# Forty-eight gathered tokens instead of thirty-two, eight tokens to a gather, and 136 sums to sort, in a two-block kernel's expert layer

## The chip, the cores and the metric

The kernel runs on one core of a Trainium2 chip (trn2), in one launch. The metric is the device time of an execution in microseconds; smaller is better. A core has a matrix engine (PE, whose weight loads are listed as PEld), a vector engine (DVE), a scalar engine (ACT), a general engine (POOL) and a queue engine (SP), each with its own instruction stream, tied together by semaphores. Transfers between memory and the on-chip buffer run on 16 DMA engines.

## The reference

Two transformer-like blocks on 256 tokens of width 2048. The change lies in the last part of the first block, the expert layer ("peer"). A token's query gives, in each of 8 heads, scores against two sets of 128 keys; the best 16 of each set are kept, the 256 pairwise sums are formed, and the best 16 sums name 16 of 16384 experts:

```python
v1, i1 = lax.top_k(s1, 16)
v2, i2 = lax.top_k(s2, 16)
cand = (v1[..., :, None] + v2[..., None, :]).reshape(T, 8, 256)
sv, si = lax.top_k(cand, 16)
expert = i1[si // 16] * 128 + i2[si % 16]
gate = softmax(sv)
a = gelu(einsum('cd,chkd->chk', x, exp_u[expert]))
out = einsum('chk,chkd->cd', gate * a, exp_v[expert])
```

`exp_u` and `exp_v` are 16384 x 2048 in float32. A token so uses 128 rows of each. The output goes back into the residual (x + g2 * out), is normalised, and enters the second block.

## The kernel before

**Weights as a stream.** All weight matrices come as units of 128 x 4096 floats (2 MB), 349 of them, in a fixed order. Behind `w_out` a unit is split into two float16 halves: SP loads it into one of two raw slots, ACT makes the high half (`hi`, L1840, two instructions), DVE the low half (`low`, L1077, two instructions), and PE multiplies (`product`, L530, L531, L532): high by high, high by low, low by high. There are two split slots: `hi` of unit n+2 waits until PE has used unit n, and PE starts unit n+2 when its `low` is done.

**Dense part.** Tokens 0 to 223 (DENSE_T = 224) go through all 16384 experts. The experts are cut into four quarters; quarter q has a stage uq (16 units, h times exp_u, gelu by ACT in `take_u`) and a stage vq (16 units, activations times exp_v, added to the residual by DVE in `residual_v`, L1573). The order is u0 u1 v0 u2 v1 u3 v2 v3. A unit is 96 matmuls of 224 columns. Gates get onto the activations by one-hot products: a routing step of 16 tokens is built by DVE (`hot`: L1547, L1549, L1553), multiplied by PE (`route`, L566, 32 matmuls), joined by DVE (`gated`, L1561), ACT (`route_high`, L2058) and DVE (`gated_low`, L1567). There are 14 steps a quarter (STEPS), one behind each of the first 14 units of u1, v0, v1 and v2. The first two `hot` of a quarter stand ahead of its stage.

**Gathered part.** Tokens 224 to 255 (ROWS_T = 32) go by gathered rows. For token i POOL issues a gather of its 128 rows of exp_u (1 MB, `row_load`, L2211) and a load that repeats its row of h on 128 partitions (1 MB, `h_load`, L2216); DVE takes the dot products (`row_dot`, L1511); ACT the gelu, DVE the weights (`row_weights`, L1519 to L1523); POOL gathers the 128 rows of exp_v, and PE sums them by four matmuls (`row_product`, L577). There is one h buffer, so `h_load(i)` waits for dot i-1. Dots lie in u2 (12, slots 2 to 13), u3 (12) and v3 (8), products in v1 (12), v2 (12) and v3 (8, from unit 6 on). At unit 12 of v3 ACT copies the sums out, PE transposes them at unit 13, and `add_rows` (DVE, L1530 to L1539) puts them into the residual at unit 14.

**Order.** Each engine's order is written out by hand: DVE's iteration n of a stage is `residual_v(n)` (v stages), `low(n+2)`, then the routing step, then (u2, u3) the dot. POOL's loads wait in order. The router's `select` runs on DVE in u0 as a generator of pieces, two or three a unit, and `top_keys` before it.

Of the kernel before, what the change touches and what calls it, by code (L numbers as in the profile page):

```python
# [54 lines left out]
ROWS_T = 32  # L55
# [129 lines left out]

def route_steps(n):

    return [n] if n < STEPS else []

ROW_GROUPS = [(0, 12), (12, 24), (24, 32)]
ROW_BATCHES = [(0, 12), (12, 24), (24, 28), (28, 32)]
ROW_LAST = {29: 0, 30: 1}


def row_loads():

    loads = []
    for n, (a, b) in enumerate(ROW_GROUPS):  # L200
        loads += [("u", i, i % 2) for i in range(a, b)]
        if n < 2:
            loads += [("v", i, i % 2) for i in range(a, b)]
        else:
            loads += [("v", i, ROW_LAST.get(i, 2)) for i in range(a, b)]
    place, count = {}, [0, 0, 0]
    for kind, i, buf in loads:
        count[buf] += 16
        place[kind, i] = (buf, count[buf])
    return place  # L210


ROW_PLACE = row_loads()
# [30 lines left out]
def program(nc, xT_d, wst, cst_d, dyn1_d, dyn2_d, dyn3_d, onehot_d, bmat_d, cmat_d, urow_d, vrow_d, skew_d, hrow_d, out_d):  # L244
    ctx = ExitStack()
    with ctx:
# [76 lines left out]
        def routed_half(q, n, r):  # L323
# [6 lines left out]
        h_row = J[0:ROWS_T, 0:2048]  # L330
        ident16 = dyn[:, 320:384].bitcast(F16)
        dots = small[:, 0:ROWS_T]
        row_w = [h_rep[:, 0:384], h_rep[:, 0:384], J[:, 6144:6272], J[:, 6272:6400]]
        row_w = [w.rearrange("p (i t) -> p i t", t=ROWS_T) for w in row_w]
        row_out = J[:, 2048:2560]
        row_tmp = J[:, 2560:3072]
        x_rows = X[:, :].rearrange("p (k t) -> p k t", k=KT)[:, :, DENSE_T:T]
# [13 lines left out]
        row_index = gates.rearrange("p q h c -> p (q h c)").bitcast(U32)[:, 0:ROWS_T]  # L351
# [3 lines left out]

        cand = J[:, 0:2048].rearrange("p (h a b) -> p h a b", h=HEADS, a=TOPK)
# [10 lines left out]
        pickT = W[:, 1024:1792].rearrange("p (f t) -> p f t", f=3)  # L367

# [3 lines left out]
        hot2 = [J[:, 4096 + 1024 * b:4096 + 1024 * (b + 1)].bitcast(F16).rearrange("p (t e) -> p t e", t=STEP_T)  # L372
                for b in range(2)]
        first1 = [J[:, 6144 + 256 * b:6144 + 256 * (b + 1)].bitcast(F16).rearrange("p (t e) -> p t e", t=STEP_T)
                  for b in range(2)]
        hot1 = [buf.bitcast(F16).rearrange("p (t r e) -> p t r e", t=STEP_T, r=2)
                for buf in (J[:, 6656:7168], dyn[:, 448:960])]
# [12 lines left out]
        def key_scores(h):  # L390
# [40 lines left out]
        row_in = [sem(f"row_in{i}") for i in range(3)]  # L431
# [4 lines left out]
            sem("rows_added"))  # L436
        merged, out_ready, relu_sb = sem("merged"), sem("out_ready"), sem("relu_sb")
# [49 lines left out]
        def _(pe_):  # L487
# [82 lines left out]
            def row_product(i):  # L570

                batch = [a <= i < b for a, b in ROW_BATCHES].index(True)
                buf, count = ROW_PLACE["v", i]
                pe_.wait_ge(row_w_ready, batch + 1)
                pe_.wait_ge(row_in[buf], count)
                for c in range(4):
                    mm = nc.tensor.matmul(psM[32 * c:32 * c + 32, 2, :], row_w[batch][:, i - ROW_BATCHES[batch][0], :],  # L577
                                          row_buf[buf][:, 512 * c:512 * c + 512], start=(i == 0), stop=(i == ROWS_T - 1))
                mm.then_inc(row_used, 1)

            def h_rows(c):
# [4 lines left out]
                for k in range(4 * c, 4 * c + 4):  # L586
                    for r in range(2):
                        mm = nc.tensor.matmul(psM[0:ROWS_T, 3, (k % 4) * P:(k % 4 + 1) * P], halves(H, k)[r][:, DENSE_T:T], ident16,
                                              start=(r == 0), stop=(r == 1))
# [362 lines left out]
            def turn_picks(qb):  # L952
                pe_.wait_ge(picked, qb + 1)
                if qb:
                    pe_.wait_ge(pickT_sb, 1)
                for f in range(3):
# [10 lines left out]
            for u in range(32):  # L967
# [3 lines left out]
                if u == 0:  # L971
                    key_head(7)
                for qb in range(2):
                    if u == 9 + 8 * qb:
                        turn_picks(qb)
                if u >= 16:
                    for step_n in route_steps(u - 16):
                        route(step_n)
                if 20 <= u < 24:
                    h_rows(u - 20)  # L980
            for q in range(4):
                v0 = FIRST[f"v{q}"]
                pe_.wait_ge(acts_ready, STEPS * (q + 1))
                for n in range(16):
# [5 lines left out]
                    if q in (1, 2) and 2 <= n < 14:  # L990
                        row_product(12 * q - 14 + n)
                    if q == 3 and 6 <= n < 10:
                        row_product(18 + n)
                    if q == 3 and n in (10, 11):
                        row_product(2 * n + 8)
                        row_product(2 * n + 9)
                    if q == 3 and n == 13:
                        pe_.wait_ge(row_out_sb, 1)
                        for j in range(4):
                            mm = nc.tensor.transpose(psM[:, 0, j * P:(j + 1) * P], row_out[:, j * P:(j + 1) * P], ident[:, :])  # L1000
                        mm.then_inc(row_T, 1)
                if q < 2:
                    stage(f"u{q + 2}", lambda s, j: unit_u(s, j), drained=False)
# [64 lines left out]
        def _(v):  # L1068
# [378 lines left out]
            def select(qb):  # L1447

                for h in range(HEADS):
                    D.put(tt(cand[:, h, :, :], val[qb][:, h, 0, :].unsqueeze(2).to_broadcast([P, TOPK, TOPK]),  # L1450
# [961 lines left out]
```

## Time and profile before

| | us |
|---|---|
| median of 3 runs (3352.15 to 3358.27) | 3352.95 |
| the profiled execution | 3353.19 |
| its span in the trace | 3351.3 |
| PE busy | 3231.2 |
| DVE busy | 2328.7 |
| ACT busy | 1236.4 |
| POOL busy | 319.9 |

The time of an execution lies about 2 us over its span. Times in the rows are microseconds from the span's start, unless marked ns. A busy PE is not PE at its peak, since matmuls are pipelined and their durations overlap; how fast it goes is read from the starts. The granted clock is a share of 2.4 GHz. The expert layer's eight stages run from 710.0 to 2029.1.

### The profile page before, as it was taken

Reading aid. Unit: us, or ns where it says so; the run is one execution under the profiler, and the core shown is the slowest. Engines: PE = TensorE matmul, PEld = TensorE weight load, DVE = VectorE, ACT = ScalarE, POOL = GpSimd, SP = SyncE. Lnnn points to the kernel's source line nnn. Section 1 sums busy time; section 2 is a strip of 40 time slices with the busy share of each in tenths; the row PEclk is TensorE's granted clock in tenths of the full one; section 3 lists DMA queues with packets and bytes.
Section 4 is the critical chain, followed back from the end, with each engine's and each line's share of the span. In section 5 each row is a group of like instructions: output and inputs, shape, how many; then the busy total and the mean of one; then the engine's idle time right before and its main releaser. Section 6 shows DMA issues by size and latency. Waiting matters only on the chain.

```text
span 3351.3 us, 70433 instructions
## 1 busy us (share of the span) xinstructions
PE 3231.2 (96%) x31230; PEld 2899.1 (87%) x31230; DVE 2328.7 (69%) x2654; ACT 1236.4 (37%) x1126; POOL 319.9 (10%) x278
## 2 busy tenths in 40 slices
PE   7999999999999999999999998999999999999998
PEld 4777768789899999999999887888888788888887
DVE  8596145799998966985698757578657655555554
ACT  2000142444444444434443324444443333343332
POOL 0275000000000002121212100210000000000000
PEclk8999999999999999999999999999999999999999
DMA  9657694446565569777978874555545455555553
GB/s 410 246 231 292 275 422 162 167 177 223 196 252 202 206 260 425 291 291 303 421 278 299 352 288 172 199 202 200 199 174 203 161 210 200 200 199 205 200 200 129
DMA packets 66046, 814.78 MB, mean 243 GB/s; under 512 B 7354, under 2 KB 9418, under 8 KB 10512
## 3 DMA queue, kind: packets, MB, share of 16 engines
q1 hardware_dynamic: 48528, 700.47, 54.8%
q0 software_dynamic: 15008, 109.10, 8.3%
q8 instruction: 174, 2.85, 0.3%
q10 hardware_dynamic: 2304, 2.10, 0.2%
q14 instruction: 32, 0.26, 0.0%
HBM read 807.71 MB, written 3.93 MB: 242 GB/s over the span
## 4 chain that ended last, share of the span: by engine, by line
PE 77%; DVE 12%; DMA 8%; issue 1%; ACT 1%; ACTq 0%; DVEq 0%; POOL 0%; SPq 0%; POOLq 0%
PE psW L530 20%; PE psW L531 20%; PE psW L532 20%; PE psW L528 7%; DMA proj<-h_rows 6%; DVE ring L1077 4%; DMA ring<-wst_dram 1%; PE psM L566 1%; PE psM L628 1%; PE psW L628 1%; DVE arena L1511 1%; PE psM L577 1%; PE psM L782 1%; DVE proj L1511 1%; DVE work L1405 1%
## 5 line engine op out<-in xcount | busy, mean ns | idle before, releaser
L1077 DVE SCALAR_TENSOR_TENSOR ring<-ring 128x2048 f16<-128x2048 f32 x526 | 1182.2, 2289 | 338.2 <-ACT ring L1840 336.3
L530 PE MATMUL psW<-h_act,ring 128*128 128x256 f16 (+1 forms) x5088 | 1366.4, 269 | 43.0 <-DVE ring L1077 20.2
L531 PE MATMUL psW<-h_act,ring 128*128 128x256 f16 (+1 forms) x5088 | 1366.1, 268 | 0.0
L532 PE MATMUL psW<-h_act,ring 128*128 128x256 f16 (+1 forms) x5088 | 1365.9, 268 | 0.0
L1840 ACT ACTIVATE ring<-ring 128x2048 f16<-128x2048 f32 x526 | 975.1, 1903 | 638.1 <-PE psW L532 548.6
L530 PE MATMUL psW<-arena,ring 128*128 128x224 f16 (+1 forms) x3072 | 812.4, 264 | 1.4 <-issue 0.9
L531 PE MATMUL psW<-arena,ring 128*128 128x224 f16 (+1 forms) x3072 | 812.2, 264 | 0.0
L532 PE MATMUL psW<-arena,ring 128*128 128x224 f16 (+1 forms) x3072 | 812.0, 264 | 0.0
L530 PEld LDWEIGHTS psW<-h_act,ring 128*128 128x128 f16 x5088 | 499.5, 98 | 99.5 <-issue 26.6
L532 PEld LDWEIGHTS psW<-h_act,ring 128*128 128x128 f16 x5088 | 500.4, 98 | 36.8
L531 PEld LDWEIGHTS psW<-h_act,ring 128*128 128x128 f16 x5088 | 499.9, 98 | 35.6
L530 PEld LDWEIGHTS psW<-arena,ring 128*128 128x128 f16 x3072 | 301.5, 98 | 41.5 <-issue 28.2
L532 PEld LDWEIGHTS psW<-arena,ring 128*128 128x128 f16 x3072 | 301.6, 98 | 12.3
L531 PEld LDWEIGHTS psW<-arena,ring 128*128 128x128 f16 x3072 | 301.5, 98 | 12.2
L528 PE MATMUL psW<-h_act,ring 128*128 128x256 f32 x896 | 202.8, 384 | 2.7 <-DVE h_act L1222 2.7
L528 PEld LDWEIGHTS psW<-h_act,ring 128*128 128x128 f32 x896 | 168.8, 191 | 32.4 <-issue 7.8
L2063 ACT ACTIVATE arena<-psW 128x448 f32<-128x448 f32 (+1 forms) x64 | 34.8, 543 | 286.2 <-PE psW L532 286.2
L1549 DVE TENSOR_TENSOR proj<-dyn,work 128x2048 f16<-128x2048 f16 x56 | 128.2, 2289 | 0.0
L2058 ACT ACTIVATE arena<-work 128x512 f16<-128x512 f32 x56 | 35.3, 630 | 222.3 <-DVE work L1561 222.3
L1783 DVE TENSOR_TENSOR work<-work 128x512 f32<-128x512 f32 x32 | 22.2, 692 | 125.5 <-ACT work L2151 125.5
L2151 ACT ACTIVATE work<-psW 128x512 f32<-128x512 f32 x32 | 19.1, 597 | 199.8 <-PE psW L532 199.8
L628 PE MATMUL psW<-ring,csilu 128*32 128x256 f32 x832 | 58.2, 427 | 24.4 <-DVE small L1183 17.5
(384 smaller groups left out, 2579.7 us busy)
## 6 DMA issues: line engine op xcount, KB each, us to landing
ring<-wst_dram SPq DMA_DIRECT2D x333, 2048.0 KB, 8.2
proj<-h_rows POOLq DMA_DIRECT2D x32, 1024.0 KB, 7.1
x_res<-xT_dram POOLq DMA_DIRECT2D x2, 2048.0 KB, 17.5
out_dram<-x_res SPq DMA_DIRECT2D x4, 512.0 KB, 2.9
bias_rows<-proj POOLq DMA_DIRECT2D x1, 1536.0 KB, 21.5
x_res<-cmat_dram POOLq DMA_DIRECT2D x1, 1024.0 KB, 7.4
x_res<-bmat_dram ACTq DMA_DIRECT2D x8, 128.0 KB, 2.7
h_act<-bias_rows ACTq DMA_DIRECT2D x8, 128.0 KB, 22.9
```

Source lines behind the costliest of these rows:

```text
L528: return nc.tensor.matmul(out, ring[:, w0:w0 + P], rhs, start=first, stop=last)
L530: nc.tensor.matmul(out, whi(s, col, P), xh, start=first, stop=False)
L531: nc.tensor.matmul(out, whi(s, col, P), xl, start=False, stop=False)
L532: return nc.tensor.matmul(out, wlo(s, col, P), xh, start=False, stop=last)
L566: mm = nc.tensor.matmul(psM[:, b, t * QUART_T:(t + 1) * QUART_T], hot2[b][:, t, :], hot1[b][:, t, r, :], start=(r == 0), stop=(r == 1))
L628: mm = nc.tensor.matmul(ada_bank(n)[32 * c:32 * c + 32, 0:256], csilu[:, k:k + 1].to_broadcast([P, 32]), ring[:, s * UNIT + k * 256:s * UN ...
L1077: ins = stt(wlo(s, c, n), ring[:, s * UNIT + c:s * UNIT + c + n], WSCALE, whi(s, c, n), ALU.mult, ALU.subtract)
L1511: v.tensor_tensor_reduce(row_buf[buf], row_buf[buf], h_rep, 1.0, 0.0, ALU.mult, ALU.add, dots[:, i:i + 1]).then_inc(dot_done, 1)
L1549: tt(hot2[b], iota16.unsqueeze(1).to_broadcast([P, STEP_T, P]), cols(1, P), ALU.is_equal).then_inc(hot2_ready, 1)
L1840: act(whi(s, p2 * (UNIT // 2), UNIT // 2), ring[:, c], ACT.Copy, scale=WSCALE).then_inc(hi_done, 1)
L2058: act(routed_half(q, n, 0), gated_w(n % 2), ACT.Copy).then_inc(route_hi, 1)
L2063: return act(A[:, span(a0, 2 * DENSE_T)].rearrange("p (m t) -> p m t", m=2), src, ACT.Gelu_apprx_tanh, scale=1 / WSCALE)
```

## The change

ROWS_T goes to 48 (now tokens 0 to 47), DENSE_T to 208 and STEPS to 13. A gather no longer takes one token's 128 rows: it takes, of 8 tokens (GROUP_T), the 16 rows of one head. One `h_load` so serves eight gathers. Products accumulate in two batches of 24 tokens. Gathers rotate through three buffers in one list; dots, gelus and products get slots from tables. The router sorts 136 sums a head: 16 with the best key of the first set, and 15 x 8 others. The list of rows comes from four small matmuls a pair of groups (`row_lists`) and `take_list`, instead of the transposed picks; h rows are taken out in units 3 to 6 of u0 instead of 4 to 7 of u1. `hot` runs on into the next quarter, so its first two steps no longer stand ahead of a stage.

```diff
-ROWS_T = 32
+PAIRS = TOPK + (TOPK - 1) * (TOPK // 2)
+ROWS_T = 48
+GROUP_T = 8
+BATCH_T = 24
...
+ROUTE_AT = [14 * k // (STEPS - 1) for k in range(STEPS)]
 def route_steps(n):
-    return [n] if n < STEPS else []
+    return [k for k, at in enumerate(ROUTE_AT) if at == n]
...
+DOT_AT = spread([("u1", 3, 15, 6), ("v0", 0, 15, 7), ("u2", 0, 15, 10), ("v1", 0, 15, 7), ("u3", 0, 15, 10),
+                 ("v2", 0, 15, 8)])
+GELU_AT = [DOT_AT[8 * g + 7] + 1 for g in range(ROWS_T // GROUP_T)]
+def products_at():
+    out, at = [], 0.0
+    for i in range(ROWS_T):
+        at = max(at + (1.75 if i < ROWS_T - GROUP_T else 1.25), GELU_AT[i // HEADS] + 1)
+        out.append(int(at))
+    return out
+EVICT_AT = [max(V3, PRODUCT_AT[BATCH_T * (b + 1) - 1] + 1) for b in range(ROWS_T // BATCH_T)]
+ADD_AT = [at + 1 for at in EVICT_AT]
+ROW_LOADS = [load[1:] for load in sorted([(at + 0.8, "u", i) for i, at in enumerate(DOT_AT)]
+                                         + [(at + 1.0, "v", i) for i, at in enumerate(PRODUCT_AT)])]
+ROW_BUFS = 3
...
+            def row_lists(b):
+                pe_.wait_ge(row_of_ready, 1)
+                for g in (2 * b, 2 * b + 1):
+                    tokens = row_of[:, P * g:P * (g + 1)]
+                    for f, src in enumerate((row_pick, pick[:, 2, :])):
+                        o = 256 * (g % 2) + P * f
+                        mm = nc.tensor.matmul(row_bank[b][:, o:o + P], tokens, src, start=True, stop=True)
+                mm.then_inc(row_ps, 1)
...
-                    cf = cand[:, h, :, :].rearrange("p a b -> p (a b)")
+                    cf = pairs[:, h, :]
...
+            def take_list(b):
+                v.wait_ge(row_ps, b + 1)
+                tmp = row_part.rearrange("p (x k) -> p x k", k=TOPK)
+                step(tt(tmp, row_bank[b]..., slot16.unsqueeze(1).to_broadcast([P, 32, TOPK]), ALU.mult))
+                step(v.tensor_reduce(rs[:, 32 * b:32 * b + 32], tmp, AX_X, ALU.add))
...
+            def rows(name, n):
+                for g in slots(GELU_AT, name, n):
+                    row_weights(g)
+                for i in slots(DOT_AT, name, n):
+                    row_dot(i)
...
+                if u == 2:
+                    row_masks()
+                if 10 <= u < 13:
+                    take_list(u - 10)
-                if u in (15, 16):
-                    hot(0, u - 15)
+                if u in (14, 15):
+                    hot(0, u - 14)
...
-            for group in range(2):
-                ra, rb = ROW_GROUPS[group]
+            h_load(0)
+            for n, (kind, i) in enumerate(ROW_LOADS):
+                if n >= ROW_BUFS:
+                    last, j = ROW_LOADS[n - ROW_BUFS]
+                    g.wait_ge(dot_done if last == "u" else row_used, j + 1)
+                    if last == "u" and j % HEADS == HEADS - 1 and j + 1 < ROWS_T:
+                        h_load(j // HEADS + 1)
+                row_load(kind, i)
```

The tables come out as follows. Dots: u1 in slots 3 5 7 10 12 15; v0 and v1 in 0 2 5 7 10 12 15; u2 and u3 in 0 1 3 5 6 8 10 11 13 15; v2 in 0 2 4 6 8 10 12 15. Products: v0 in 4 5 7 9 11 12 14; u2 in 0 5 6 8 10 12 13 15; v1 in 1 3 4 6 8 10 11 13 15; u3 in 3 4 6 8 10 11 13 15; v2 in 1 2 4 6 8 9 11 13; v3 in 1 2 3 4 6 7 8 9. Routing steps stand behind units 0 1 2 3 4 5 7 8 9 10 11 12 14. The sums are copied out at units 0 and 10 of v3 and added at 1 and 11.

## Rows read from the trace of the kernel before

**Rows 1.** The page: the chain that ended last, share of the span by engine.

```profile
PE 77%; DVE 12%; DMA 8%; issue 1%; ACT 1%; ACTq 0%; DVEq 0%; POOL 0%; SPq 0%; POOLq 0%
```

**Rows 2.** Windows, u0 u1 v0 u2 v1 v3: us, busy by engine, PE clock, DMA share, GB/s.

```profile
710.00:871.30 161.30, 152.96 (x1558) 149.57 (x1558) 156.03 (x289) 74.73 (x59) 0.00 (x0) 0.99 0.56 208
871.30:1041.10 169.80, 164.13 (x2022) 162.25 (x2020) 152.88 (x128) 77.34 (x68) 6.33 (x4) 0.98 0.60 221
1041.10:1203.10 162.00, 160.19 (x1987) 159.35 (x1985) 149.48 (x132) 68.63 (x48) 0.00 (x0) 0.99 0.57 209
1203.10:1353.70 150.60, 148.02 (x1535) 146.36 (x1533) 98.66 (x57) 66.47 (x47) 28.86 (x23) 1.00 0.90 368
1353.70:1527.30 173.60, 171.95 (x2083) 161.32 (x2084) 151.66 (x136) 68.53 (x49) 35.98 (x14) 1.00 0.77 287
...
1851.30:2029.10 177.80, 161.76 (x1604) 150.46 (x1601) 121.03 (x133) 60.06 (x36) 17.01 (x21) 0.94 0.81 309
```

**Rows 3.** Timeline of PE between two units of v1: start, us, engine, line, operation.

```profile
1440.17 0.95 PE L566 MATMUL psM<-dyn,proj 128*128 128x32 f16 x32
1441.06 1.06 PE L577 MATMUL psM<-proj 128*32 128x512 f32 x8
1442.05 0.27 PE L530 MATMUL psW<-arena,ring 128*128 128x224 f16 x1
```

**Rows 4.** Timeline of PE, 56 matmuls of 224 columns, then 30 of 256: first, last.

```profile
1699.83 0.26 PE L530 MATMUL psW<-arena,ring 128*128 128x224 f16 x1
...
1705.10 0.26 PE L531 MATMUL psW<-arena,ring 128*128 128x224 f16 x1
...
2099.83 0.27 PE L530 MATMUL psW<-h_act,ring 128*128 128x256 f16 x1
...
2102.99 0.27 PE L532 MATMUL psW<-h_act,ring 128*128 128x256 f16 x1
```

**Rows 5.** Timeline of DVE over an iteration of v1: low, routing step, next residual.

```profile
1431.28 4.49 DVE L1077 SCALAR_TENSOR_TENSOR ring<-ring 128x2048 f16<-128x2048 f32 x2 [1.03 <-ACT ring L1840]
1435.69 0.68 DVE L1561 SCALAR_TENSOR_TENSOR work<-psM,arena 128x512 f32<-128x512 f32 x1
...
1440.90 0.45 DVE L1573 SCALAR_TENSOR_TENSOR x_res<-psW,mod,x_res 128x224 f32<-128x224 f32 x1
```

**Rows 6.** Timeline of u3: ACT's high half; DVE's dot and the low behind it.

```profile
1601.36 3.70 ACT L1840 ACTIVATE ring<-ring 128x2048 f16<-128x2048 f32 x2
...
1602.24 2.29 DVE L1511 CUSTOM_DVE_ANT_0 arena<-arena,proj 128x2048 f32<-128x2048 f32 x1 [3.16 <-DMA proj<-h_rows]
...
1604.46 4.49 DVE L1077 SCALAR_TENSOR_TENSOR ring<-ring 128x2048 f16<-128x2048 f32 x2
```

**Rows 7.** DMA issues, KB, us to landing: whole run; 1400 to 1500; 1240 to 1340.

```profile
proj<-h_rows POOLq DMA_DIRECT2D x32, 1024.0 KB, 7.1
...
proj<-vrow_dram,gates POOLq DMA_INDIRECT x5, 7.8
...
ring<-wst_dram SPq DMA_DIRECT2D x10, 2048.0 KB, 10.5
proj<-urow_dram,gates POOLq DMA_INDIRECT x5, 11.8
```

**Rows 8.** Waits of PE in v3: us in total, times, longest.

```profile
PE psM L577 <- DMA proj<-vrow_dram,gates: 8.2, 1, 8.2
PE psM L577 <- DVE proj L1523: 7.2, 1, 7.2
```

**Rows 9.** Window of u0 right behind a wait of PE.

```profile
812.50:818.00 5.50, 5.45 (x40) 4.83 (x41) 5.29 (x18) 2.00 (x2) 0.00 (x0) 0.69 0.81 286
```

**Rows 10.** DVE groups, 738 to 880: a search over 256 elements, and over 128.

```profile
L1459 DVE FIND_INDEX8 proj<-proj 128x8 uint32<-128x256 f32 x16 | 6.7, 419 | 0.0
...
L1445 DVE FIND_INDEX8 arena<-arena,work 128x8 uint32<-128x128 f32 x1 | 0.3, 285 | 0.0
```

**Rows 11.** Timeline of DVE: the last residual of v3, behind `add_rows`.

```profile
2031.85 0.45 DVE L1573 SCALAR_TENSOR_TENSOR x_res<-psW,mod,x_res 128x224 f32<-128x224 f32 x1
```

More of the change, by code:

```diff
@@ L183, with spread, slots @@
 SSM_SUM_TURN = 9
+ROUTE_AT = [14 * k // (STEPS - 1) for k in range(STEPS)]
 def route_steps(n):
-    return [n] if n < STEPS else []
[L192 to L213, printed above, removed]
+    return [k for k, at in enumerate(ROUTE_AT) if at == n]
+ORDER = ["u0", "u1", "v0", "u2", "v1", "u3", "v2", "v3"]
+def spread(plan):
+    out = []
+    for name, first, last, count in plan:
+        x0 = 16 * ORDER.index(name)
+        out += [x0 + first + (i * (last - first)) // max(1, count - 1) for i in range(count)]
+    return out
[7 more added lines that the diff above has]
+        out.append(int(at))
+    return out
+PRODUCT_AT = products_at()
+assert len(DOT_AT) == ROWS_T
+V3 = 16 * ORDER.index("v3")
+EVICT_AT = [max(V3, PRODUCT_AT[BATCH_T * (b + 1) - 1] + 1) for b in range(ROWS_T // BATCH_T)]
+ADD_AT = [at + 1 for at in EVICT_AT]
+assert ADD_AT[1] < V3 + 15
+def slots(table, name, n):
+    return [i for i, at in enumerate(table) if at == 16 * ORDER.index(name) + n]
+ROW_LOADS = [load[1:] for load in sorted([(at + 0.8, "u", i) for i, at in enumerate(DOT_AT)]
+                                         + [(at + 1.0, "v", i) for i, at in enumerate(PRODUCT_AT)])]
+ROW_BUFS = 3
+ROW_PLACE = {load: (n % ROW_BUFS, 16 * (n // ROW_BUFS + 1)) for n, load in enumerate(ROW_LOADS)}
 class Chain:
@@ L975, in _ @@
                         turn_picks(qb)
+                if u == 9:
+                    for b in range(3):
+                        row_lists(b)
                 if u >= 16:
@@ L989, in _ @@
                         route(STEPS * (q + 1) + step_n)
[L990 to L1001, printed above, removed]
-                if q < 2:
-                    stage(f"u{q + 2}", lambda s, j: unit_u(s, j), drained=False)
+                    for i in slots(PRODUCT_AT, f"v{q}", n):
+                        row_product(i)
+                    for b in slots(ADD_AT, f"v{q}", n):
+                        turn_out(b)
+                if q < 2:
+                    u0 = FIRST[f"u{q + 2}"]
+                    for n in range(16):
+                        s = slot_ready(u0 + n, 0, 0)
+                        pe_.wait_ge(bank_free, u0 + n + 1)
+                        unit_u(s, n % 4).then_inc(w_used, 1)
+                        for i in slots(PRODUCT_AT, f"u{q + 2}", n):
+                            row_product(i)
             two_sums()
@@ L1599, in _ @@
                     gated(0, n)
-                    if n + 2 < STEPS:
-                        hot(0, n + 2)
+                    hot(0, n + 2)
                     gated_low(0, n)
+                if u >= 16:
+                    rows("u1", u - 16)
             for q in range(1, 4):
                 v0 = FIRST[f"v{q - 1}"]
-                for n in range(2):
-                    hot(q, n)
-                if q > 1:
-                    row_weights(q - 2)
                 for n in range(16):
@@ L1642, in _ @@
                     low(FIRST["v3"] + j + 2)
-                if j < 8:
-                    row_dot(24 + j)
-                if j in (5, 9):
-                    row_weights(2 + (j == 9))
-                if j == 14:
-                    add_rows()
+                rows("v3", j)
+                for b in slots(ADD_AT, "v3", j):
+                    add_rows(b)
             inverse_rms(4)
```

282 lines of the change are left out of this document (152 added, 130 removed).

## The prediction

> **What bounds the kernel now.** The sum is made against the profiled execution, 3353.2 us, 0.2 us over the median of the runs; a change is to be told from none beyond 0.2%, 7 us. I read the page's chain first: PE carries 77% of it, DVE 12%, DMA 8% [rows 1]. Then the stages: u0 161.3 us, u1 169.8, v0 162.0, u2 150.6, v1 173.6, v3 177.8 [rows 2]; u3 and v2 repeat u2 and v1 within 0.1. The reader should see three kinds. In v1 PE is busy throughout: a unit, a routing step (1441.06 - 1440.17 = 0.89 us) and a product (0.99 us) follow without a gap [rows 3]. In u0 DVE is busy 156 of 161 us. In u3 (and u2) a unit lasts 9.86 us where PE needs 9.2, because the dot waits 3.16 us for the repeated h row [rows 6], and each such load starts only behind the last dot and takes 7.1 us [rows 7]. In v3 the same chain of loads comes late, and PE stands 7.2 us for weights and 8.2 us for a gather [rows 8].
>
> **What a unit costs PE.** 56 matmuls of 224 columns start within 5.27 us, 95.8 ns each; 30 of 256 within 3.16 us, 109.0 ns [rows 4]. The difference, 13.2 ns for 32 columns, is 0.41 ns a column. At 208 columns I take 95.8 - 16 x 0.41 = 89.2 ns, so a unit of 96 goes from 9.20 to 8.56 us, and 128 units lose 82 us of PE work. The four routing steps dropped save 4 x 0.8 = 3.2 us (0.8 a step where no product follows; 0.89 in [rows 3]). Sixteen more products cost 16 x 1.09 = 17 us (0.99 to 1.09).
>
> Here a rule speaks against me. The Trainium skill, page "TensorE: Matmul & The Clock Gate", section "Back-to-back issue gap", has the spacing of a stream of load and matmul pairs set by both, 81 ns at 128 columns and 131 at 512. By it the 16 columns would be worth 2.1 ns, not 6.7, and 26 us, not 82. The rows' slope contradicts it.
>
> **What DVE costs.** An iteration with a routing step is: low 4.41 us (1431.28 to 1435.69), step 5.21 (to 1440.90), residual 0.38 and a wait of 1.03 for ACT [rows 5]: 10.0 of work. PE's unit with a step shrinks to 8.56 + 0.8 = 9.36, so DVE becomes the longer one there; a dot adds 2.22 (1602.24 to 1604.46, [rows 6]), 12.2. Relief: three units of 16 have no step (4.8). DVE can run late by 8.56 - 1.95 (high half) - 4.41 = 2.2 us before PE waits. A v stage sums on DVE to 16 x 4.8 + 13 x 5.2 + 7 x 2.2 = 160 us; on PE to 137 + 10.4 + 7 to 9 products, 155 to 157.
>
> **Stage by stage.** I go through the units, each engine starting at the later of its own end and what it waits for. PE's work after + its waits:
> - u0 and u1, now 331.1. DVE is the chain. The searches shrink: 419 ns at 256 elements, 285 at 128 [rows 10], so at 136 about 0.13 x 5 x 8 x 2 heads = 9 to 10 us; the pair sums give 2.5. Added: masks 1.6, three lists 4.4, index fixing and row numbers 2.3. Net -4. But in six units DVE falls below PE's 8.6 to 9.2 (h rows, now in u0, 0.65 each) and idles, 3 us. The row lists on PE (under 3 us) hide in the 4.41 us of the low behind the picks; without that cover they cost 3. `hot(0, 1)` only moves from unit 16 to 15. In u1 eleven later steps and six dots make 133 us of DVE against 128 of PE, with waits of 1.0, 2.5, 0.8 and 2.5. Sum 330 (324 to 334).
> - v0, now 162.0: 155.0 of PE. Product 0, in slot 4, needs weights that DVE makes at the end of its iteration 3, which lags a unit: 8.3 us. Products 2 and 5 stand two slots behind the dot whose buffer their gather takes: 2.2 and 1.5. The clock 1.8 (below). 169.
> - u2, now 150.6: 145.7. The h wait goes. But product 9, slot 6, needs a gather that waits for dot 16, slot 5: that dot ends 0.44 + 1.86 + 4.41 + 2.22 = 8.9 us behind unit 5, about when unit 6 ends, and the gather takes 7.8 us, as those of v1 did [rows 7]. PE waits 7.7, and the clock. Five more products stand two slots behind: 2 x 8.56 = 17.1 against 8.9 + 0.3 + 7.8 = 17.0, nothing to 1 each. 154.
> - v1, now 173.6: 157.2 of PE, 6 of waits where dots and steps meet. 163.
> - u3, like u2 (product 29 behind dot 36): 155. v2: 156.1 + weights 2 + gathers 3.7 + clock 3: 165.
> - v3, now 177.8: no dots. 137 + 8 x 1.09 + turning 1.2 = 147. `add_rows` is split, 4.4 us each, in iterations 1 and 11, where DVE has 2 us of room.
> - Behind v3: the last residual now starts at 2031.85 [rows 11], 2.8 after the stage's end, since `add_rows` stands before it. That goes: -2.9.
>
> The queues: SP issues 128 raw loads as before. POOL has 96 gathers and 6 h loads instead of 64 and 32, spread over 112 units, so 2 MB + about 0.9 MB in 9.3 us, some 330 GB/s against 368 in u2 [rows 2]; I cost that at nothing for the raw loads, whose cover is the unit before. A dot never waits for a gather by my slots (9 us or more of room).
>
> The clock: behind a wait of 2.3 us the window has a mean granted clock of 0.69, part at 1.2 and part at 2.4 GHz, and 40 matmuls in 5.5 us where 57 fit [rows 9]: 1.6 us lost. I take 1.8 a long wait; nothing where DVE leads, 1.8 for each wait over 1 us as the other end (+8 in all).
>
> Sum: -1 + 7 + 3.5 - 10.5 + 4.5 - 8.5 - 31 - 3 = -39, so **3315 us**. So of 82 us of columns half is given back to waits; the largest gain is the removed chain of v3.
>
> Unknown costs. A gather's landing: 7.8 beside raw loads, 11.8 beside h loads [rows 7]. Each microsecond above 7.8 costs about 9 us in all, since some twenty products stand one or two slots behind; 7.8 is nearest, the DMA share being nearer v1's. Below, 7 us would give 2. Lists, masks and searches, whose only rows are those of the nearest sizes: -2 to +6.
>
> **The rivals.**
> - *The waits dissolve* (0.12). If DVE catches up behind each PE wait and the landings are short, v0 to v2 run at PE's work: 46 us less, 3269. For: v1 is now wholly PE's [rows 2]. Against: DVE's 160 us against 155.
> - *The gathers land late* (0.09), slower. Two queues now load throughout; u2's landings of 11.8 and raw loads of 10.5 us [rows 7] become the rule. From 9 us up every product two slots behind its buffer waits; at 11.3 the gain is gone, at 11.8 the stages give about 49 us back: 3364. For: 330 GB/s. Against: v1's 7.8 at 287.
> - *The spacing stops at 95.8 ns* (0.04), slower. A weight load might bound the pairs. Then units stay at 9.2 and I get 3363. Against: 32 matmuls of a routing step, each with its own weights, go in 0.89 us [rows 3], 28 ns each. Between the two (0.03), with the loads taking half of what the columns give, a spacing of 92.5 ns, the unit is 8.9 us; of the 0.32 us a unit, 41 us, some 24 reach the end, as 48 of 82 do above: 3339. The rule of the Trainium skill named above would be of this kind.
> - *More time at half clock and more short waits than I count* (0.14): 3330 to 3346.
> - That the change does not do what it says: the 136 sums hold every candidate of the best 16, and the shapes follow from the constants; no chance of its own.
>
> **How the numbers follow.** Forecast 3315 with 0.58 for 3290 to 3330. The range takes in the fourth rival and part of the first: 3282 to 3346; what lies outside is most of the first and the slow ends. Faster by over 0.2%: the forecast, the first, the fourth and the case between, and a part of the late gathers, 0.86; slower 0.10 from the late gathers (0.06) and the stopped spacing (0.04); the same 0.04, landings near 11 us.
>
> **What would show it.** 208-column matmuls starting 89.2 ns apart; v3 near 147 us without a gap; u2 and u3 with one wait of PE on a gather each, near 8 us; v0 longer than before, with a wait for `row_weights`; DVE over 95% busy in v0; no DVE wait for h rows; gathers landing at 8 us. Wrong if v0, v1 and v2 sum far from 497 us, if many products wait, or if dots wait for gathers.

## The result, and the profile after

The changed kernel takes 3371.13 us (median of 4 runs, 3364.93 to 3374.86) against 3354.26 us of the kernel before on the same chip: a ratio of 1.0054, interval 1.0040 to 1.0068. I had forecast 3315 us, faster. It is slower by 0.5%.

The page of the changed kernel (profiled execution 3364.93 us): its span, the first row of busy times, the chain that ended last by engine, POOL's DMA queue (packets, MB, share of 16 engines), and the issues of the h loads (count, KB, median us to landing).

```profile
span 3363.2 us, 70461 instructions
...
PE 3179.2 (95%) x31258; PEld 2825.2 (84%) x31258; DVE 2336.3 (69%) x2673; ACT 1235.3 (37%) x1132; POOL 302.5 (9%) x284
...
q0 software_dynamic: 16656, 115.53, 9.7%
...
PE 67%; DVE 20%; DMA 8%; issue 3%; ACT 2%; ACTq 0%; POOL 0%; DVEq 0%; SPq 0%; POOLq 0%
...
proj<-h_rows POOLq DMA_DIRECT2D x6, 1024.0 KB, 17.6
```

PE is busy for 52 us less (3179.2 against 3231.2; the forecast's own terms, 82 and 3 less and 17 more, come to 68), and yet the span is 12 us longer. PE's share of the chain fell from 77% [rows 1] to 67%. The last line is the one that I had not priced: the h loads land in 17.6 us, those of before in 7.1 [rows 7].

The windows of the eight stages after, u0 to v3 in their order (the answer to [rows 2]; same columns):

```profile
712.30:869.50 157.20, 147.34 (x1614) 144.07 (x1611) 149.05 (x297) 76.84 (x63) 0.56 (x1) 0.99 0.59 216
869.50:1043.10 173.60, 156.40 (x1958) 153.43 (x1955) 165.15 (x134) 73.85 (x62) 17.84 (x9) 0.95 0.70 251
1043.10:1213.50 170.40, 158.07 (x2011) 150.23 (x2009) 159.75 (x141) 67.42 (x47) 19.73 (x15) 0.97 0.79 283
1213.50:1380.00 166.50, 147.61 (x1594) 138.52 (x1592) 96.11 (x58) 66.09 (x48) 22.26 (x18) 0.95 0.85 322
1380.00:1548.60 168.60, 159.04 (x2026) 149.40 (x2024) 158.92 (x140) 67.53 (x47) 24.70 (x17) 0.98 0.84 309
1548.60:1716.00 167.40, 149.26 (x1602) 138.88 (x1600) 96.19 (x58) 65.86 (x48) 17.70 (x19) 0.95 0.85 317
1716.00:1894.90 178.90, 159.78 (x2027) 150.16 (x2026) 154.55 (x135) 67.64 (x47) 26.34 (x18) 0.95 0.82 293
1894.90:2044.10 149.20, 147.03 (x1610) 138.24 (x1607) 111.04 (x126) 64.19 (x41) 6.34 (x7) 1.00 0.73 276
```

Read the first number behind each pair of times (the stage's length) beside PE's busy time. In v3 the two lie 2.2 us apart. In u2, u3 and v2 they lie 18 to 19 us apart: PE stands.

Its waits between 700 and 2070 (us in total, times, longest) say for what:

```profile
PE psM L608 <- DMA proj<-vrow_dram,rs: 45.1, 8, 16.2
...
PE psW L561 <- DVE ring L1128: 34.4, 22, 4.3
PE psM L608 <- DMA arena<-vrow_dram,rs: 17.3, 3, 16.7
DVE arena L1589 <- DMA proj<-h_rows: 16.7, 2, 8.6
PE psM L608 <- DVE h_act L1600: 9.4, 3, 8.3
...
DVE proj L1589 <- DMA proj<-h_rows: 3.9, 1, 3.9
```

PE waits 62 us for gathered rows of exp_v, with two waits above 16 us, where the longest that I had counted on was 8; and DVE waits 20.6 us for h loads, where I had said none. How the two hang together can be followed through one unit of u2 in the timeline (start, us; behind [ the idle time before, and its releaser):

```profile
1261.90 0.65 POOL L2328 DMA_DIRECT2D proj<-h_rows  x1 [18.20 <-DVE rs L1589]
...
1284.42 2.29 DVE L1589 CUSTOM_DVE_ANT_0 arena<-arena,proj 128x2048 f32<-128x2048 f32 x1 [8.06 <-DMA proj<-h_rows]
...
1286.99 2.76 POOL L2323 DMA_INDIRECT arena<-vrow_dram,rs  x1 [22.18 <-DVE rs L1589]
...
1294.55 1.92 PE L608 MATMUL psM<-arena,h_act 128*24 128x512 f32 x8 [16.71 <-DMA arena<-vrow_dram,rs]
```

The h load is issued at 1261.90 and lands 22.4 us later; dot 16 waits for it and frees its buffer at 1286.7; only then can the gather for product 9 start; PE, ready since 1277.8, gets its rows at 1294.5. Such a chain stands behind an h load in four places: from the last matmul of one unit to that of the next, units 7 of u2, 4 of v1, 5 of u3 and 2 of v2 (counted from 0) take 28.8, 18.4, 20.7 and 29.0 us. With the h load of one row (below) they take 20.3, 10.4, 9.7 and 12.6, together 44 us less; and the eight stages (1331.8 us) are 49 longer than the 1283 that my forecasts add up to.

In this unit the DMA engines are never idle while the load is under way, but they move little. A window of the changed kernel in that stretch (the last two numbers: DMA share, GB/s); up to 1272 POOL's queue is nearly alone on the engines, behind it the next raw load joins in:

```profile
1267.00:1277.00 10.00, 10.00 (x111) 8.98 (x109) 4.49 (x2) 4.23 (x3) 0.00 (x0) 1.00 1.00 224
```

Other steps came out as written. 101 matmuls of 208 columns, first and last, in the timeline of PE:

```profile
1550.53 0.25 PE L562 MATMUL psW<-h_act,ring 128*128 128x208 f16 x1
...
1559.45 0.25 PE L563 MATMUL psW<-h_act,ring 128*128 128x208 f16 x1
```

8.92 us over 100 steps is 89.2 ns, the forecast figure, and a search over 136 sums (DVE groups, 738 to 880) takes 294 ns where 256 took 419 [rows 10]:

```profile
L1513 DVE FIND_INDEX8 proj<-proj 128x8 uint32<-128x136 f32 x16 | 4.7, 294 | 0.0
```

And the two waits that I had priced at 8.3 us (weights of product 0 in v0) and 7.7 us (the gather behind a dot one slot earlier, in u3) stand in PE's timeline at 8.31 and 7.73:

```profile
1099.49 1.92 PE L608 MATMUL psM<-proj,h_act 128*24 128x512 f32 x8 [8.31 <-DVE h_act L1600]
...
1677.66 1.92 PE L608 MATMUL psM<-proj,h_act 128*24 128x512 f32 x8 [7.73 <-DMA proj<-vrow_dram,rs]
```

### The profile page after: what moved, and what is told of

Read it like the earlier page. It is cut to its first block, busy times and chain, and to the rows that moved or that the text cites. A ratio compares the mean times of both kernels' runs of the same rounds, so it can differ in the third digit from the quotient of the medians.

```text
span 3363.2 us, 70461 instructions
## 1 busy us (share of the span) xinstructions
PE 3179.2 (95%) x31258; PEld 2825.2 (84%) x31258; DVE 2336.3 (69%) x2673; ACT 1235.3 (37%) x1132; POOL 302.5 (9%) x284
## 3 DMA queue, kind: packets, MB, share of 16 engines
q0 software_dynamic: 16656, 115.53, 9.7%
## 4 chain that ended last, share of the span: by engine, by line
PE 67%; DVE 20%; DMA 8%; issue 3%; ACT 2%; ACTq 0%; POOL 0%; DVEq 0%; SPq 0%; POOLq 0%
PE psW L561 17%; PE psW L563 17%; PE psW L562 17%; DVE ring L1128 9%; PE psW L559 7%; DMA proj<-vrow_dram,rs 4%; DMA ring<-wst_dram 3%; PE psW L677 1%; ACT ring L1935 1%; PE psM L677 1%; DVE proj L1589 1%; PE psM L831 1%; PE psM L608 1%; DVE dyn L1647 1%; DVE arena L1643 1%
## 5 line engine op out<-in xcount | busy, mean ns | idle before, releaser
L561 PE MATMUL psW<-arena,ring 128*128 128x208 f16 (+1 forms) x3072 | 798.6, 260 | 6.7 <-DVE ring L1128 5.7
L562 PE MATMUL psW<-arena,ring 128*128 128x208 f16 (+1 forms) x3072 | 798.3, 260 | 0.0
L563 PE MATMUL psW<-arena,ring 128*128 128x208 f16 (+1 forms) x3072 | 798.1, 260 | 0.0
L2158 ACT ACTIVATE arena<-psW 128x416 f32<-128x416 f32 x64 | 33.0, 516 | 291.8 <-PE psW L563 291.8
L608 PE MATMUL psM<-proj,h_act 128*24 128x512 f32 x240 | 36.1, 676 | 54.1 <-DMA proj<-vrow_dram,rs 45.1
## 6 DMA issues: line engine op xcount, KB each, us to landing
proj<-h_rows POOLq DMA_DIRECT2D x6, 1024.0 KB, 17.6
```

What stands on the lines that cost most here:

```text
L561: nc.tensor.matmul(out, whi(s, col, P), xh, start=first, stop=False)
L562: nc.tensor.matmul(out, whi(s, col, P), xl, start=False, stop=False)
L563: return nc.tensor.matmul(out, wlo(s, col, P), xh, start=False, stop=last)
L608: mm = nc.tensor.matmul(psM[32 * c:32 * c + BATCH_T, 2 + i // BATCH_T, :], row_w[:, 8 * (g % 4) + h, :], row_buf[buf][:, 512 * c:512 * c + ...
```

## The experiments

What is new about the h load is its source. Before, one row of h goes to all 128 partitions (`[[0, P], [1, D_MODEL]]`); now eight rows, each repeated 16 times, come from a source of three dimensions, 8 outermost. The bytes are the same. Below, "the layer" is the time from the last matmul of the query projection to the first behind v3: 1329.3 us before, 1339.7 after. What comes behind it took 1309.5 to 1312.4 us in every profiled execution, but its start lay anywhere from 707 to 717 us, and the layer leaves both out. It is of one execution of each kernel, though, and that one can lie off the median: 6 us below it for the change, 8 us above it for e12_sixteen_rows, 9 us below it for e5_both. Where the two measures differ by as much, the median of the whole time decides. Ratios are against the kernel before.

### One row, as before

```diff
-g.dma_start(h_rep, bass.AP(hrow_d.tensor, i * GROUP_T * D_MODEL, [[D_MODEL, GROUP_T], [0, TOPK], [1, D_MODEL]]))
+g.dma_start(h_rep, bass.AP(hrow_d.tensor, i * GROUP_T * D_MODEL, [[0, P], [1, D_MODEL]]))
```

> Each of the six h loads reads one row for all 128 partitions, the form of before; the h rows of a group's other seven tokens are left out, so 42 of the 48 gathered tokens get wrong dots. All else is the changed kernel. Theory A (the loads of eight rows, each repeated 16 times, are slow themselves and hold up the gathers queued behind them on POOL's queue and the raw loads beside them): the loads land in 7 to 9 us instead of 15 to 22, the gathers behind them in 8 to 14 instead of 20 to 29, the four long units (u2.7, v1.4, u3.5, v2.2, together 45 us over my forecast) shrink by some 40 us, and the kernel takes 3315 to 3330 us. Theory B (POOL's and SP's queues together load the DMA engines too much, whatever the form): bytes are the same, so the time stays within 7 us of the changed kernel, 3360 to 3375. Theory C (DVE is the bound of the stages with dots): no change either, and no wait of PE goes.

3320.54 us, ratio 0.9909 (0.9889 to 0.9928); the layer 1294.8. The four units last 20.3, 10.4, 9.7 and 12.6 us, 44 us less than in the changed kernel. In the stretch behind the h load of u2 the same DMA engines, just as busy, move twice as much:

```profile
1262.00:1267.00 5.00, 5.00 (x54) 3.98 (x53) 1.02 (x1) 3.36 (x3) 0.00 (x0) 1.00 1.02 433
```

Theory A holds; B and C fall, since bytes, queues and DVE's work are the same. (The page of this run has no landing for the h loads, so the expected 7 to 9 us can't be laid against a number.)

### A gather in place of the load

```diff
+g.iota(h_index[:, :], pattern=[[P, ROWS_T // GROUP_T]], base=0, channel_multiplier=1).then_inc(h_index_made, 1)
...
+step(ts(h_index[:, :], h_index[:, :], 4, None, ALU.logical_shift_right))
...
-g.dma_start(h_rep, bass.AP(hrow_d.tensor, i * GROUP_T * D_MODEL, [[D_MODEL, GROUP_T], [0, TOPK], [1, D_MODEL]]))
+g.indirect_dma_start(h_rep, None, hrow_d[:, :],
+                     bass.IndirectOffsetOnAxis(ap=h_index[:, i:i + 1], axis=0))
```

> The six h loads become gathers from the DRAM rows of h, with a row number for each partition (8 g + p // 16, one iota and one shift), so that all 128 partitions get what the changed kernel gives them; nothing is left out. Theory A: a gather of 128 rows of 8 KB lands as the other gathers do, 7 to 12 us, and the kernel takes 3315 to 3330 us, less than both kernels. Theory A2 (what is slow is that eight rows of h are read 16 times each, whatever asks for them): the loads still land in 15 to 22 us and the time stays at 3360 to 3375. Theory B: 3360 to 3375.

3322.97 us, ratio 0.9917 (0.9899 to 0.9936); the layer 1295.0. Not to be told from the run above, though here every partition gets its own token's h. Reading eight rows 16 times each is not slow; how it was asked for was. Its windows of u2, v1, u3 and v2:

```profile
1208.30:1366.80 158.50, 146.40 (x1595) 137.90 (x1592) 96.08 (x58) 66.08 (x48) 21.54 (x18) 0.97 0.85 337
1366.80:1530.40 163.60, 157.90 (x2027) 149.09 (x2025) 158.45 (x139) 67.63 (x47) 23.62 (x17) 1.00 0.84 318
1530.40:1687.40 157.00, 148.54 (x1603) 138.99 (x1600) 96.15 (x58) 65.74 (x48) 21.55 (x19) 0.97 0.85 339
1687.40:1852.70 165.30, 159.46 (x2027) 149.92 (x2025) 154.44 (x135) 67.52 (x47) 23.54 (x18) 0.99 0.84 321
```

These are nearly the stages that I had forecast: 158.5, 163.6, 157.0 and 165.3 against 154, 163, 155 and 165, eight stages of 1287 against 1283 us.

### Only the form, in the kernel before

```diff
-g.dma_start(h_rep, bass.AP(hrow_d.tensor, i * D_MODEL, [[0, P], [1, D_MODEL]])).then_inc(h_rep_in, 16)
+g.dma_start(h_rep, bass.AP(hrow_d.tensor, i // 8 * 8 * D_MODEL, [[D_MODEL, 8], [0, 16], [1, D_MODEL]])).then_inc(h_rep_in, 16)
```

> The kernel before, with one thing of the change alone: its 32 h loads (still one for each gathered head of a token) read eight rows, each repeated 16 times, in place of one row for all 128 partitions; most dots get the h of other tokens. Same bytes, same waits. If the form is slow by itself, wherever it stands: the loads land in 14 us or more instead of 7.1, each of the dots of u2, u3 and v3, which wait for their load now, waits 7 us or more longer, so u2 and u3 go from 150 to above 220 us each and the kernel above 3480 us. If the form is slow only in the changed kernel's order (a gather straight behind it, the gathers spread over all stages): landing 7 to 9 us and 3345 to 3370 us.

3637.35 us, ratio 1.0847 (1.0822 to 1.0872). u2 and u3 take 250.1 and 254.6 us instead of 150.6 and 150.4. Its page has the landing, its waits of DVE from 1200 to 2330 the price (75.8 us in total in the kernel before):

```profile
proj<-h_rows POOLq DMA_DIRECT2D x32, 1024.0 KB, 16.7
```

```profile
DVE proj L1511 <- DMA proj<-h_rows: 205.2, 16, 16.0
DVE arena L1511 <- DMA proj<-h_rows: 153.3, 13, 13.7
```

The form is slow in the old order too, and where a dot waits for each load, 32 of them cost 284 us. The packets of POOL's queue grow from 15008 to 19104, 128 a load.

### Other orders of the same bytes: 16 x 8, 8 pieces, 4 rows, 2 rows, 16 rows

Four edits of the source's dimensions (the rest is the changed kernel), and one that cuts the load in eight plain ones (a dot then waits for eight completions a group):

```diff
-i * GROUP_T * D_MODEL, [[D_MODEL, GROUP_T], [0, TOPK], [1, D_MODEL]]
+i * GROUP_T * D_MODEL, [[0, TOPK], [D_MODEL, GROUP_T], [1, D_MODEL]]       (e3_order)
+i * GROUP_T * D_MODEL, [[2 * D_MODEL, 4], [0, 2 * TOPK], [1, D_MODEL]]     (e10_four_rows)
+i * GROUP_T * D_MODEL, [[4 * D_MODEL, 2], [0, 4 * TOPK], [1, D_MODEL]]     (e11_two_rows)
+6 * i * D_MODEL,       [[D_MODEL, TOPK], [0, GROUP_T], [1, D_MODEL]]       (e12_sixteen_rows)
```

```diff
+for t in range(GROUP_T):
+    g.dma_start(h_rep[TOPK * t:TOPK * (t + 1), :],
+                bass.AP(hrow_d.tensor, (i * GROUP_T + t) * D_MODEL, [[0, TOPK], [1, D_MODEL]]))     (e7_eight)
```

> The h load reads the same eight rows, but as 16 passes over the eight rows instead of eight runs of 16 copies, so neighbouring partitions get different rows (partition p the h of token p mod 8 of the group: most dots are wrong). Still a source of three dimensions. If the three dimensional source alone makes it slow (it is cut in pieces, each with packets of its own): landing 15 us or more and 3360 to 3375 us, perhaps more since there are 16 pieces and not eight. If it is the runs of 16 copies of one row on neighbouring partitions: landing 7 to 9 us and 3315 to 3330 us.

> The changed kernel with each h load of eight rows written as eight direct loads of 16 partitions, each with one row (the same bytes to the same places, nothing left out). If the slow landing comes of the cut in eight pieces of 16 partitions (the load of the changed kernel shows some 128 more 4-byte packets than a load of one row): the pieces land late as well, 15 us or more from the first issue, gathers behind them too, and POOL spends 7 us on the issues: 3360 to 3385. If it comes of the one instruction's three dimensional source: each piece lands in a few us, the last about 9 to 11 us from the first issue, and the kernel takes 3325 to 3345.

> The changed kernel, its h loads reading four rows, each repeated 32 times (most dots get the h of another token of the group); same bytes, a source of three dimensions. If the number of pieces counts (four of 32 partitions instead of eight of 16): half the extra packets (some 48 a load over the form of one row), landing 10 to 13 us, 3335 to 3352. If any cut makes it slow: 3360 to 3375. If only pieces as small as the 16 DMA engines are slow: as e1_one_row, 3313 to 3325.

> As e10_four_rows, with two rows, each repeated 64 times. If the number of pieces counts: 16 extra packets a load, landing 8 to 10 us, 3320 to 3335. If any cut makes it slow: 3360 to 3375. If only pieces as small as the 16 DMA engines are slow: 3313 to 3325.

> The changed kernel, its h loads reading 16 rows, each repeated 8 times (wrong h for most partitions; same bytes, a source of three dimensions with 16 outermost where the changed kernel has 8). Looking back, e10_four_rows and e11_two_rows were slower the fewer rows they read, 3435 and 3466 us, and the last stretch of their loads shows a DMA share of 0.22 to 0.25 and 0.12 to 0.14, that is 4 and 2 engines of 16. Theory F (the outermost count is the number of DMA engines that a direct load of this form gets): with 16 it gets all of them, no packets of 4 bytes beyond those of e1_one_row (15888 in POOL's queue), landing 7 to 11 us, 3315 to 3337. Theory G (distinct rows, or any source of three dimensions, make it slow, and e3_order was spared for another reason): at least as slow as the changed kernel, 3360 or more. The Trainium skill, page DMA: Bandwidth & Descriptors, section Why a DMA increments its semaphore by 16 and not by 1, has a rule of the kind of theory F: the largest number up to 16 that divides the slowest sizes of both sides.

The packets are those of POOL's queue on each page; "extra" is what is over the 15888 of the kernel with one row, divided by six loads.

| h load | us | ratio (interval) | layer | packets | extra a load |
|---|---|---|---|---|---|
| one row | 3320.54 | 0.9909 (0.9889 to 0.9928) | 1294.8 | 15888 | 0 |
| gather | 3322.97 | 0.9917 (0.9899 to 0.9936) | 1295.0 | 15888 | 0 |
| 16 outermost, 16 rows | 3331.55 | 0.9944 (0.9927 to 0.9960) | 1313.7 | 15888 | 0 |
| 16 outermost, 8 rows in turn | 3334.18 | 0.9947 (0.9928 to 0.9966) | 1305.0 | 15888 | 0 |
| 8 loads of 16 partitions | 3343.64 | 0.9973 (0.9962 to 0.9984) | 1317.7 | 16560 | 112 |
| 8 outermost (the change) | 3371.13 | 1.0054 (1.0040 to 1.0068) | 1339.7 | 16656 | 128 |
| 4 outermost | 3435.42 | 1.0240 (1.0218 to 1.0262) | 1415.3 | 18192 | 384 |
| 2 outermost | 3466.40 | 1.0339 (1.0317 to 1.0361) | 1443.5 | 21264 | 896 |

I had expected fewer rows to be better, on the thought that each row is a piece with a price of its own. It is the other way round: of 16, 8, 4 and 2 outermost, each is slower than the one before. 3435.42 and 3466.40 us lie above all three ranges that I had given for either run. Late in the load of u2, when PE stands and DVE waits for h, the DMA share counts the engines at work. Four outermost (POOL's queue and what is left of a raw load):

```profile
1304.00:1310.00 6.00, 0.00 (x0) 0.00 (x0) 0.00 (x0) 3.71 (x2) 0.00 (x0) 0.50 0.25 107
```

Two outermost (four fifths of the packets are of POOL's queue):

```profile
1318.00:1338.00 20.00, 0.00 (x0) 0.00 (x0) 1.75 (x1) 2.87 (x2) 0.00 (x0) 0.50 0.13 54
```

A share of 0.25 is 4 engines of 16, one of 0.13 is 2; a quarter and an eighth of 433 GB/s are 108 and 54, and 107 and 54 are moved. The packets fit too, exactly: if k engines carry the 128 rows, each has 128 / k; sixteen engines with as many entries each make 2048 / k, and 2048 / k - 128 is 128, 384 and 896 for k = 8, 4 and 2, and 0 for 16. (That the engines without a share are filled up with packets of 4 bytes is my reading of these counts.) The 8 of the change can be seen as well, where an h load runs with no raw load beside it. Two such windows of the changed kernel, behind the issues at 1089.31 and 1404.12:

```profile
1091.00:1093.50 2.50, 0.18 (x8) 0.07 (x3) 2.50 (x2) 0.00 (x0) 1.43 (x1) 1.00 0.44 111
1406.20:1408.20 2.00, 2.00 (x26) 2.00 (x24) 2.00 (x2) 0.00 (x0) 1.70 (x2) 1.00 0.52 131
```

Shares of 0.44 and 0.52 fit 8 engines of 16 (windows so short cut through packets at their edges). The rate does not lie on the series of the other two: half of 433 would be 216 GB/s, and 111 and 131 are moved. (Four outermost, with POOL's queue alone at work from 1091.5 to 1093 and from 1436 to 1438, move 66 and 86, also less than in the late stretch above.) e12_sixteen_rows was the test of the count: 16 outermost, no extra packets, 3331.55 us. Theory F holds, G falls.

The Trainium skill has this rule, page "DMA: Bandwidth & Descriptors", section "Why a DMA increments its semaphore by 16 and not by 1": the number of engines is the largest up to 16 that divides the slowest size of both access patterns. These runs agree, with the shares of 0.25 and 0.13 and the packet counts above.

The count of engines is not all. With 16 outermost the kernel is still 11 to 14 us over the one with one row, though there are no extra packets. e3_order landed its h loads in 10.2 us in the median, and its 3334.18 us lie between its two ranges. A window right behind the second h load, in which POOL's queue is alone on the engines, first of e12_sixteen_rows, then of the kernel with one row:

```profile
1089.00:1092.00 3.00, 0.00 (x0) 0.00 (x0) 3.00 (x3) 0.24 (x1) 0.79 (x1) 1.00 1.01 224
1087.00:1091.00 4.00, 0.16 (x7) 0.06 (x3) 4.00 (x5) 0.62 (x2) 1.39 (x1) 1.00 0.95 375
```

The h load and the gather behind it keep all 16 engines busy in both, at 224 GB/s in the one and 375 in the other; the 111 and 131 GB/s of the change are low for eight engines in the same way. e7_eight, whose pieces are plain, moves 127 GB/s at a share of 1.02 from 1089 to 1093. It lies in its second range (3325 to 3345) but pays about half of the loss, with one more completion on each engine for each further piece (7 x 16 = 112 packets, my reading of the count). So a direct load of these forms has a second price, beyond the number of its engines. What it comes from is open. These loads may hand the partitions to the engines in another pattern than the load of one row does; no run tried that by itself.

### The router alone

The kernel before with the 136 sums (the pair sums, the searches over `pairs`, the index of the second key put right), nothing else.

> The kernel before with one part of the change alone: the router sorts 136 sums of a head instead of 256. My step put the shorter searches at 9 to 10 us of DVE and the pair sums at 2.5 us, less four added short instructions (about 1 us), all in u0 where DVE is the chain: u0 from 161.2 to about 151 to 153, the kernel 3343 (3340 to 3348). Rival: PE's units of 9.2 us take over in the units that hold the searches, and only half of it arrives: 3348 to 3351.

3344.53 us, ratio 0.9983 (0.9973 to 0.9992): 3 to 9 us less. u0 by its window:

```profile
713.10:869.40 156.30, 151.48 (x1557) 150.07 (x1556) 145.34 (x284) 74.69 (x58) 0.00 (x0) 0.99 0.58 214
```

DVE's busy time in u0 falls by 10.7 us (from 156.03, [rows 2]) and the stage by 5.0. The rival had the mechanism right, that only half arrives: in the units that hold the searches PE's 9.2 us take over as soon as DVE is shorter. But 3344.53 us lies outside its range (3348 to 3351) and in the one of the main line (3340 to 3348), which had counted on 8 to 10 us in u0. The profiled execution took 3350.38 us, 6 over the median, so the trace does not show where the rest of the gain lies.

### Other slots for the products, with and without the gather

On the kernel with the gathered h, the slots of the 48 products from a written table; then the dots' as well:

```diff
-PRODUCT_AT = products_at()
+PRODUCT_AT = [37, 38, 40, 40, 42, 43, 46, 51, 55, 57, 57, 60, 62, 64, 65, 67, 68, 70, 70, 72, 73, 74, 77, 78,
+              83, 84, 87, 89, 92, 94, 96, 97, 99, 99, 102, 103, 105, 105, 107, 109, 114, 114, 117, 118, 119, 120, 122, 122]
```

> The gathered h of e2_h_gather, and the 48 products put in other slots of the same stages (a written table in place of the rule of 1.75 slots; dots and everything else stay): no product stands closer than some 2.5 slots behind the dot whose buffer its gather takes, most at two units with a dot or a step in them, and the first stands a slot later. Theory D (what is left of the waits of e2_h_gather is the distance between a gather and its product: 13.0 + 9.9 us of PE on gathers, 10.8 us on weights, plus PE's half clock behind each): these waits fall below 8 us in all, u2 and u3 go to 145 to 150 us, v0 to 158 to 164, the kernel to 3275 to 3292. Rival E (DVE is the chain in v0 to v2, so PE's waits turn into waits for the ring's low halves): at most 10 us go, 3310 to 3323.

> As e4_slots, but the 48 dots are moved as well: several go where no routing step stands and some units take two or three, so that dots and steps no longer meet in one unit where DVE already needs more time than PE. Theory D with DVE as the next bound: another 8 to 15 us go, 3262 to 3282. If DVE's total per stage is what counts and not how it is spread: same as e4_slots within 5 us. If two gathers for neighbouring slots get in each other's way: slower than e4_slots, above 3292.

> The changed kernel with the product slots of e4_slots alone; the h loads stay as in the changed kernel (direct, eight rows repeated 16 times). Theory A and D together: the slots take away the waits on gathers that land in 8 to 10 us, but the gathers behind an h load still land 20 to 29 us after their issue, so part of the 45 us stays: 3300 to 3335, 20 to 45 us above e4_slots. If the slots alone were the fault and the load's form of no account: as e4_slots, 3275 to 3292.

e4_slots: 3290.43 us, ratio 0.9820 (0.9803 to 0.9836), the layer 1267.7, 27 us less than with the old slots. Its waits of PE, 700 to 2010, and its windows of u2 and u3, where PE is now busy for 143.3 of 143.3 and 143.7 of 145.2 us:

```profile
PE psW L564 <- DVE ring L1131: 36.1, 23, 4.3
...
PE psM L611 <- DMA arena<-vrow_dram,rs: 3.8, 1, 3.8
PE psM L611 <- DMA proj<-vrow_dram,rs: 3.8, 3, 2.2
```

```profile
1201.80:1345.10 143.30, 143.30 (x1587) 137.61 (x1585) 96.25 (x58) 65.75 (x48) 18.66 (x17) 1.00 0.91 360
1509.50:1654.70 145.20, 143.74 (x1587) 137.42 (x1585) 96.14 (x58) 66.09 (x48) 21.62 (x17) 1.00 0.91 361
```

The 34 us of waits on gathers and weights (13.0, 9.9 and 10.8) shrink to 7.6 on gathers and none on weights: theory D. What remains is the wait for the ring's low halves, DVE's. The kernel lies in the expected 3275 to 3292, u2 (143.3) a little below its 145 to 150, v0 (165.8 us) above its 158 to 164.

e5_both: 3287.71 us, ratio 0.9811 (0.9794 to 0.9827), the layer 1257.1, 11 us shorter still. But that execution, 3278.93 us, is 9 us below its own median. By the whole time the two can't be told apart, as the second line of the expectation has it (within 5 us); by the stages, one execution each, moving the dots gives v0 157.8 and v2 157.2 us (165.8 and 166.4 in e4_slots) and loses 10 again in u3 (155.7 against 145.2), where a product waits 4.0 us for its gather and raw loads come late. The median lies above the 3262 to 3282 of the first line. These are the fastest kernels of this study, 1.8 and 1.9% under the kernel before, and they compute all that the changed kernel does.

e8_slots_direct, the new slots with the change's own h load: 3350.76 us, ratio 0.9995 (0.9985 to 1.0004). Better than the changed kernel by 20 us, but 60 us behind e4_slots, where I had expected 20 to 45 (3300 to 3335 us): dots stand 21.8 us for h, PE 53.2 for gathers, 15.9 us the longest. Better slots can't hide a load that holds up the queue behind it.

## Why the prediction was wrong

**The step that failed** is in "The queues": "POOL has 96 gathers and 6 h loads instead of 64 and 32 ... I cost that at nothing". I counted loads and bytes. I never asked whether a load of the new form lands like one of the old, though the diff shows a new source, and took 7.1 us [rows 7] without a word. It measured 17.6, and 14.6 to 22.4 for the six; gathers queued right behind one landed in 20 to 29 us. Nor was there a bound for it among the unknown costs, whose landings of gathers I bounded at 7.8 and 11.8 from loads of the old form. With the gathered h in its place, the stages sum to 1287 us for my 1283; with it, 1332. Some of that closeness is luck: u0 and u1 came 5 us under my figure, the other six 9 over theirs.

The Trainium skill speaks against this load in the section named above, and again in "Rules for kernel authors": an outermost size under 16 confines a transfer to at most that many engines. I had not looked for a rule on the one operation whose shape changed. By it the change has half the engines for 1 MB; at 433 GB/s for all sixteen, an estimate from the window of e1_one_row, that is 4.8 us alone instead of 2.4. The change's own stretches, 111 and 131 GB/s, make it 8 to 9, so the rule alone would have priced the load too low as well.

Point by point:

- *The spacing*: right, 89.2 ns. The Trainium skill's rule, page "TensorE: Matmul & The Clock Gate", section "Back-to-back issue gap", would have made 16 columns worth 2.1 ns, an estimate from its two figures; the traces have 95.8 ns at 224 and 89.2 at 208, and the measurement decides.
- *u0 and u1*, 330 (324 to 334): 330.8, but u1 has an h load in it; with the gathered h 324.8, the lower end (1.6 of the 6 us lie in u0, where there is no h load). The router alone shortens u0 by 5 us.
- *v0*, 169: 170.4; with the gathered h 169.7. The weights' wait 8.31 for 8.3. DVE's busy time 159.75 for 160. The sign "DVE over 95% busy in v0" did not fit that figure: 160 of 169 is under 95%, and it came to 94%.
- *u2, u3*, 154 and 155: 166.5 and 167.4 with the load, 158.5 and 157.0 without it. Of the two waits of 7.7 us on the gathers behind dots 16 and 36, u3's measured 7.73 and u2's, with the gathered h, 9.69.
- *v1, v2*, 163 and 165: 168.6 and 178.9; without it 163.6 and 165.3. v0, v1 and v2, 497 together, sum to 518, and to 499 without it.
- *v3*, 147: 149.2, and without the load 148.0. The chain of loads is gone, 29 us, the largest gain as forecast.
- *Behind v3*, -2.9: the last residual starts at 2044.27, 0.2 us behind the window's end, not 2.8 [rows 11]. Right, and of the 2.9 us 2.3 reach PE: its first matmul behind v3 starts 8.0 us after the last of v3, 10.3 before.
- *DVE waits for no h row*: wrong, 20.6 us. *Gathers land at 8 us*: 8.2 to 10.2 in the median, but not behind an h load.
- *The slow rival, "the gathers land late"*: it named the symptom (twenty products one or two slots behind, stages giving 49 us back, 3364) and the wrong cause. Two queues throughout are no burden: with the same bytes and 337 GB/s in u2 the gathered h gives 3323. Its condition was a landing of 11 us everywhere; what came was 15 to 22 us for six h loads and 20 to 29 us for gathers right behind them. I gave it 0.09, and 0.06 of that to slower.
- *The sum*: its terms, -39 on 3353.2, make 3314, not 3315, which changes nothing.
- *The waits dissolve*, 3269: not by itself, but with slots chosen for it 3290 and 3288.

## What to carry to other kernels

When a change gives a transfer another access pattern, price it as a new operation even if its bytes are the same: look at the outermost sizes of both sides, and give the landing a bound of its own. If one of them is small and not the partitions, try a gather by an index instead; here that gave the time of the load with one row. A slow transfer costs most through the queue behind it, here a gather, its buffer and a product, so read landings one by one beside the issues ahead of them, not as a median. And a slot rule (1.75 units a product) should be laid against the distance from the freeing dot to the product's gather: moving products by up to three slots took 27 us off the layer here.

## What the runs showed of the hardware

- A direct load on POOL's queue of 128 partitions from a source with k = 8, 4 or 2 outermost runs on k of the 16 DMA engines: shares of 0.25 and 0.13 and 107 and 54 GB/s for 4 and 2, 0.44 and 0.52 and 111 and 131 GB/s for 8. The queue's packets grow by 2048 / k - 128 a load.
- Such a load with 16 outermost keeps all engines busy and still moves 224 GB/s where a load of one row moves 375 (e12_sixteen_rows and e1_one_row, POOL's queue alone).
- While the change's h load in u2, the gather behind it and the next raw load are under way, the DMA share reads 1.00 and the rate 224 GB/s (1.02 and 433 in the same unit with the load of one row). A full DMA share is no sign of a full rate.
- A gather of eight rows, 16 times each, in place of a direct load of one repeated row leaves the kernel as fast: 3322.97 against 3320.54 us.
- Six times eight direct loads of 16 partitions cost the kernel 19 to 21 us more than six gathers of 128 (by the ratios and by the medians).
